# Modulation sections 3 and 4 as VectorE row sums in the gate stage instead of TensorE matmuls in the second attention

## What is computed

```
ua = (ya * silu(ga)) @ w_up_a        # the same for b and c
gates = sigmoid(gm.reshape(B, S, 3, D))
merged = gates[:, :, 0] * ua + gates[:, :, 1] * ub + gates[:, :, 2] * uc
x = x + merged @ w_o
```

```
mod = silu(c) @ ada_w[layer] + ada_b[layer]       # 1024 x 6144
shift_m, scale_m, gate_m, shift_f, scale_f, gate_f = split(mod, 6)
h = rms_norm(x) * (1 + scale_m) + shift_m
x = x + gate_m * mixer(h)
h = rms_norm(x) * (1 + scale_f) + shift_f
x = x + gate_f * conv_ffn(h)
```

## Time and profile before

| | |
|---|---|
| median of 3 runs | 1063.72 us |
| the profiled execution's own time | 1063.48 us |
| its span | 1061.7 us |
| TensorE matmul busy | 1043.2 us, 98% |
| VectorE busy | 774.5 us, 73% |
| ScalarE busy | 582.5 us, 55% |
| loads of the SyncE queue | 215.41 MB |
| granted TensorE clock | 0.998 of full speed |

### The profile page before, as it was taken

How to read it: one execution, slowest core, us unless ns; L and a number is a source line. 1 busy time by engine, 2 the same in 40 slices (tenths; PEclk the granted TensorE clock), 3 DMA queues, 4 the chain that set the end, 5 groups by cost and what they waited for, 6 DMA issues and landing times.

```text
span 1061.7 us, 21412 instructions
## 1 busy us (share of the span) xinstructions
PE 1043.2 (98%) x9022; PEld 997.1 (94%) x9022; DVE 774.5 (73%) x1138; ACT 582.5 (55%) x889; POOL 67.5 (6%) x78
## 2 busy tenths in 40 slices
PE   8999999999999999999999999999999999999997
PEld 8988889999999999897788999999899999999996
DVE  6467777765576768987867999977688769677642
ACT  6555666565446675534757555533545456565432
POOL 2000000000010614000110000000000010000000
PEclk9999999999999999999999999999999999999999
DMA  8756757566755674444667898867768676555621
GB/s 267 217 182 235 238 162 233 180 188 184 243 163 165 194 221 157 130 149 151 212 220 244 283 290 274 287 245 289 258 219 287 202 233 204 188 170 189 229 80 40
DMA packets 166956, 220.29 MB, mean 207 GB/s; under 512 B 4514, under 2 KB 147262, under 8 KB 166861
## 3 DMA queue, kind: packets, MB, share of 16 engines
q1 hardware_dynamic: 165338, 215.41, 62.2%
q0 software_dynamic: 832, 1.65, 0.8%
q10 hardware_dynamic: 690, 1.86, 0.5%
HBM read 217.80 MB, written 1.11 MB: 206 GB/s over the span
## 4 chain that ended last, share of the span: by engine, by line
PE 81%; DVE 13%; ACT 3%; issue 2%; DMA 0%; SPq 0%; DVEq 0%; ACTq 0%
PE psG L584 19%; PE psG L586 19%; PE psG L585 19%; DVE wlo L1883 4%; PE psS L584 4%; PE psS L586 4%; PE psS L585 4%; PE psG L739 1%; DVE arow L1960 1%; PE psG L712 1%; PE psG L714 1%; PE psG L725 1%; PE psS L874 1%; PE psX L890 1%; DVE fz L2459 1%
## 5 line engine op out<-in xcount | busy, mean ns | idle before, releaser
L1883 DVE TENSOR_TENSOR wlo<-raw,whi 128x1024 fp32r<-128x1024 f32 x309 | 373.6, 1246 | 100.5 <-ACT whi L1270 94.7
L584 PE MATMUL psG<-Hlo,whi 128*128 128x256 f32 x1420 | 404.7, 285 | 2.1 <-DVE Hlo L1924 0.9
L586 PE MATMUL psG<-Hhi,whi 128*128 128x256 f32 x1420 | 400.2, 282 | 0.0
L585 PE MATMUL psG<-Hhi,wlo 128*128 128x256 f32 x1420 | 399.9, 282 | 0.0
L1270 ACT CAST whi<-raw 128x1024 fp32r<-128x1024 f32 x309 | 312.2, 1048 | 116.6 <-DMA raw<-in_ffn_w_down_dram 29.9
L584 PEld LDWEIGHTS psG<-Hlo,whi 128*128 128x128 f32 x1420 | 268.3, 189 | 6.0 <-issue 3.4
L585 PEld LDWEIGHTS psG<-Hhi,wlo 128*128 128x128 f32 x1420 | 268.5, 189 | 0.0
L586 PEld LDWEIGHTS psG<-Hhi,whi 128*128 128x128 f32 x1420 | 268.3, 189 | 0.0
L584 PE MATMUL psS<-Glo,whi 128*128 128x256 f32 x316 | 89.8, 284 | 0.0
L586 PE MATMUL psS<-Ghi,whi 128*128 128x256 f32 x316 | 89.1, 282 | 0.0
L585 PE MATMUL psS<-Ghi,wlo 128*128 128x256 f32 x316 | 89.1, 282 | 0.0
(11 more groups left out here) (454 smaller groups left out, 1779.1 us busy)
## 6 DMA issues: line engine op xcount, KB each, us to landing
raw<-in_ada_w_dram SPq DMA_DIRECT2D x48, 1024.0 KB, 5.6
raw<-in_ffn_w_up_dram SPq DMA_DIRECT2D x44, 1024.0 KB, 5.2
raw<-in_w_in_dram SPq DMA_DIRECT2D x28, 1024.0 KB, 6.6
raw<-in_ev_w_in_dram SPq DMA_DIRECT2D x26, 1024.0 KB, 5.5
raw<-in_ffn_w_down_dram SPq DMA_DIRECT2D x22, 1024.0 KB, 4.9
raw<-in_od_w_in_dram SPq DMA_DIRECT2D x12, 1024.0 KB, 7.8
raw<-in_w_in_dram SPq DMA_DIRECT2D x11, 512.0 KB, 6.7
raw<-in_w_o_dram SPq DMA_DIRECT2D x4, 1024.0 KB, 5.1
```

Source lines behind the costliest of these rows:

```text
L584: mm(o, a_hi, b_lo, start=first, stop=False, skip_group_check=shared)
L585: mm(o, a_lo, b_hi, start=False, stop=False, skip_group_check=shared)
L586: return mm(o, a_hi, b_hi, start=False, stop=last, skip_group_check=shared)
L1883: V.tensor_tensor(ring_half(wlo, v, h - H0[v]), src, ring_half(whi, v, h - H0[v]).bitcast(F32), ALU.subtract).then_inc(lo_split, 1)
```

## The change

Sections 3 and 4 join `ON_VECTOR`. Their eight units move from the second attention to the gate stage, one behind the up unit of each branch from a1 to b3 (gate1a to gate3b). `add_rows` gets a parameter: its first operation on a unit stands ahead of the branch's multiply, its second behind the branch's add. The spreads, copies and sums of the two sections are placed at the end of the gate stage and in w_o, and the old matmuls, copies, folds and sums go. Rows of the sections now lie in `arow0`.

```diff
-ON_VECTOR = (2, 5, 6, 7, 8, 9)
+ON_VECTOR = (2, 3, 4, 5, 6, 7, 8, 9)
...
-              2: ("slot8", "slot9", "slot10", "slot11"), 3: ("hg7a", "hg7b", "na0a", "na1a"),
-              4: ("na2a", "na3a", "na4a", "na4b"), 7: ("up0.9", "up0.10", "fd0.0", "fd0.2"),
+              2: ("slot8", "slot9", "slot10", "slot11"), 3: ("gate1a", "gate1b", "gate1c", "gate2a"),
+              4: ("gate2b", "gate2c", "gate3a", "gate3b"), 7: ("up0.9", "up0.10", "fd0.0", "fd0.2"),
...
             section(f"up_{br}{i}", "U" if br != "b" else "V", f"w_up_{br}", i * 256, 1)
+            ada(f"gate{i}{br}")
...
+                    elif (i, br) == (3, "a"):
+                        pe.wait_ge(turned_kept, 8)
+                        spread(3)
+                    elif (i, br) == (3, "b"):
+                        sum_ada(3)
+                    elif (i, br) == (3, "c"):
+                        spread(4)
...
                 project(u, Whi, Wlo, ready=(merge_ready, 0) if n == 0 else None)
+                if n == 1:
+                    sum_ada(4)
...
-                if n == 0:
-                    pe.wait_ge(pT_kept, NT0 + 2 * NA)
-                    sum_ada(3)
-                elif n == 1:
-                    sum_ada(4)
...
-            def add_rows(place):
+            def add_rows(place, ks=range(2)):
...
-                    for k in range(2):
+                    for k in ks:
...
                         if k == 0:
                             step(ins)
-                    then(ins, row_added, ON_DVE.index(u) + 1)
+                        else:
+                            then(ins, row_added, ON_DVE.index(u) + 1)
...
+                    add_rows(f"gate{i}{br}", (0,))
                     dve.wait_ge(gate_e, n + 1)
                     v = gate[:, n % 2, :, :]
                     dve.wait_ge(half_used, H0[u] + NH[u])
...
                         step(V.tensor_tensor(merged[:, :, :], merged[:, :, :], mt[:, :, :], ALU.add))
+                    add_rows(f"gate{i}{br}", (1,))
...
-            for n in (3, 4):
-                fold_row(n)
```

More of the change, by code:

```diff
@@ L403, in ada_row @@
         def ada_row(n):
-            if n == 3:
-                return qke[:, 1, :, :].rearrange("p h s -> p (h s)")
-            return arow0[:, n % 2, :] if n < 3 else arow1[:, ROW[n], :]
-        ROW = {4: 0, 7: 0, 5: 2, 6: 3, 10: 4, 8: 5, 9: 0, 11: 1}
+            return arow0[:, ROW[n], :] if n < 5 else arow1[:, ROW[n], :]
+        ROW = {0: 0, 1: 1, 2: 0, 3: 0, 4: 1, 7: 0, 5: 2, 6: 3, 10: 4, 8: 5, 9: 0, 11: 1}
         def output_bank(n):
@@ L1520, in _ @@
                         keep_spread(2)
+                    elif (i, br) == (3, "b"):
+                        keep_spread(3)
                     elif (i, br) == (1, "b"):
@@ L1544, in _ @@
                 nc.scalar.copy(Hhi[:, 2 * n:2 * n + 2, :], cxT[:, 2 * n:2 * n + 2, :]).then_inc(vhi_set, 2)
+                if n == 0:
+                    keep_spread(4)
             for g in range(4):
@@ L2157, in _ @@
                                             ).then_inc(ctx_scaled, 1)
+                    elif (i, br) == (3, "c"):
+                        keep_ada(SUM_IX[3] + 1)
+                    add_rows(f"gate{i}{br}", (0,))
                     dve.wait_ge(gate_e, n + 1)
@@ L2182, in _ @@
                 dve.sem_inc(x_ready, 1)
+                if n == 2:
+                    keep_ada(SUM_IX[4] + 1)
             def renorm(i, gain, tiles=range(KT)):
@@ L2441, in _ @@
                     add_last(u, 0, 2, lambda: dve.wait_ge(tile_done, 1))
-                if n == 0:
-                    keep_ada(SUM_IX[3] + 1)
-                elif n == 1:
-                    keep_ada(SUM_IX[4] + 1)
+                if n == 1:
                     step(V.scalar_tensor_tensor(cm[:, 2, :], mod[:, 0, 32:40, 0], 1.0, pcol[:, C_FFN:C_FFN + 8],
```

## The result

The changed kernel takes 1094.42 us in the median of 5 runs (1094.24 to 1096.54), the kernel before in the same job 1063.6 us (5 runs, 1063.41 to 1063.92). The ratio is 1.0294, 95% interval 1.0283 to 1.0305: 30.8 us slower, where 25.8 were forecast. The time lies in the predicted range.

A forecast was written before the change was run, and what follows sets the result against it. TensorE bounds the gate stage, VectorE the second attention's start. A slot-release loop adds 25.9 us, the other terms net -0.1: 1063.48 + 25.8 = 1089.3, made 1089.5 us against the runs' median; range 1080 to 1101.

The forecast's parts named there:

- gate stage, to c3's multiply: Seven slower turns, then c3's split and up unit, put c3's multiply at 316.6 instead of 290.74: +25.9 us.
- sum 4 and spread 4 around w_o: One sum returns between two w_o units (+0.45 us); the second new spread stands ahead of w_o, TensorE full (+0.6).
- the attention's units: Eight units leave the second attention's start; of 8.4 us of TensorE work only 0.25 us is gained.
- two sums out of the projection: Sums of sections 3 and 4 leave the output projection behind the attention, 0.45 us each: -0.9 us.
- everything behind: Behind c3's multiply in the gate stage TensorE is bound by itself again and gives nothing back.
- The loop: Gate stage: gate unit's load waits for the slot freed by a modulation unit's second operation at branch's end; seven turns, 90.2 us.
- The size of a turn: Gate stage: load, ScalarE's high part, splits, operations, multiply, add: 12.9 us, 12.2 in branch a, 14.2 in c1; before, 8.57.
- rival 4: Gate stage: loop exists and loads share engines with up and modulation units: 7 x 2.6 us more, about 1107; chance 0.10.
- The end of the loop: After the seventh turn at 312.4, up unit c3's split (1.25) and 2.85 us on TensorE precede c3's multiply at 316.6.
- The attention: Second attention's start: VectorE's softmax steps set the pace, modulation matmuls stand in its pauses; removing them gains 0.25 us.

The follow-up runs named there:

- the second profile: The changed kernel run again with no edit, for another profile: median 1094.64 us, ratio 1.0293 to the kernel before.
- the small fillers of the experiment: Kernel before the change, products of sections 3 and 4 cut from eight of 256 columns to four of 8 per unit: 1063.6 us, ratio 1.0006.

## Why the prediction held, and where it was off

The account goes by the second profile (1094.81 us, against 1063.48 of the profiled execution before, +31.3):

| term | predicted | measured |
|---|---|---|
| gate stage, to c3's multiply | +25.9 | +31.1 (321.85 - 290.74) |
| sum 4 and spread 4 around w_o | +1.05 | +1.2 (525.02 - 492.74 = 32.3, less 31.1) |
| the attention's units | -0.25 | +0.1 (550.70 - 518.28 = 32.4) |
| two sums out of the projection | -0.9 | -0.8 (589.98 - 558.39 = 31.6) |
| everything behind | 0 | -0.3 |

**The loop** was right, in kind and in place. The slot decides: with slots of their own the loss falls to 3.1 us, and one operation a branch moved past two others changes 9.0 us where 9.4 were reckoned. Seven loads, each issued 0.02 to 0.04 us behind the second operation's end, are in the trace.

**The size of a turn** is where the prediction put the load in with 5.27 us each. "Here the gate unit is at the head of its turn, so I take 5.2" fails: the up unit's load, issued 0.4 us behind, and the modulation unit's, 1.3 to 2.8 us behind, take a share of the engines, and the mean is 5.8. That is 3.8 us in seven turns (40.7 - 36.9), and holding these loads back shortened the seven by 3.4 and returned 2.6 us of time. Which of the two loads takes how much was not tried. The whole is rival 4 at a fifth of its price. Part was given back: the operation on a section's first unit, a plain multiply, takes 0.75 instead of 1.28 us. From 222.2 to the seventh turn's end it was 92.9 us instead of 90.2, so +2.7.

**The end of the loop** was reckoned as a split and an up unit behind it, 4.2 us, and took 6.8: +2.6, the other half of the miss. The prediction left out that the gate unit of c3 too is behind the sum of section 3, which waits for ScalarE's copy behind a sigmoid, and that TensorE comes out of that wait at the 1.2 GHz level. "The granted clock is 1.00 in both windows, which is the 2.4 GHz level, so it has no part in the sum" was read from the kernel before, and the change itself brought the idle times. The stretch hangs on the load over ScalarE and TensorE: it is 14.3 us from the first copy of the last gate unit to c3's multiply, with long and with short operations on VectorE. Moving the copy and filling the wait brought 0.9 us each by the rows (6.8, 5.9, 5.0) and 1.1 and 1.2 us of time, the latter inside the spread of the runs. 0.8 us stay without an experiment.

**The attention** was right: VectorE sets the pace, and the units were filler. The kernel before without their products takes the same time. The gain of 0.25 us did not show in the two profiles of the changed kernel, but in others. From the attention's first row (psY<-hv,attm) to the block behind it was 25.54 us before and 25.12 with the small fillers of the experiment, both at a mean clock of 1.00 over 25.5 us. The twelve profiles of kernels without these units show 0.87 or 0.93. Seven of them take 25.1 us there (0.93), the changed kernel 25.9 (0.87) and 25.7 (0.93), and the two longest 25.9 and 26.0 (0.87). In the first profile a group of four scores took 1.23 us instead of 0.70. That the slower products cost time only where VectorE waits for them is argued, not shown. That the clock is lower without the units is in every profile; whether their products or their loads keep it up was not tried by itself.

**The first profile** was that of the slowest of its five runs. Its third load took 7.17 us (6.54 in the second), and the -0.9 us of the two sums are missing in it, since the sum of squares waited 1.08 us for GpSimd. That wait is not in the second.

## What to carry to other kernels

A prefetch ring turns the end of one consumer into the start of another's load: for every unit added, look which one lies a ring's length ahead, when its slot comes free, and whether the engine that frees it also has to work on the new load; if so, sum that loop against the period of the stage. Inside such a loop each operation ahead of the release counts once a turn, so an operation moved behind it pays several times its length. And matmuls in another engine's pauses cost nothing here, so moving them away gave next to nothing, and what the new place costs came on top.

## What the runs showed of the hardware

- A load of a megabyte over SyncE's queue, alone on the engines, took 5.23 to 5.43 us from issue to the first use on ScalarE. With half a megabyte issued 0.4 us behind and a megabyte 1.3 to 2.8 us behind (at the last, w_o's), it took 5.3 to 6.2; with the half as two parts of 256 KB (branch b's up unit), 6.5 to 7.2 and 5.9 to 6.1. With a megabyte issued 4.6 us ahead and the loads behind held back, it took 6.35 and 7.6; with one issued 5.0 to 6.8 us ahead, 5.3 to 5.8.
- At the end of the stage TensorE came out of waits of 2.7 and 3.5 us at the 1.2 GHz level: some 15 of its next products followed by 0.21 us instead of 0.12. Inside the turns, where the load is waited for, more work on TensorE cost nothing; on the way out of the stage the level cost about 1 us, and idle products in the wait kept the clock up.
- A product of a tile with a column (TENSOR_SCALAR, 128x1024) took 0.75 us on VectorE, the same with an addition (SCALAR_TENSOR_TENSOR) 1.28.
